# RWKV scan on one core: the carried state taken as one 128-column product per pair of heads

## The reference, cut to what matters

```
def wkv7_scan(r, decay, k, v, a, b):
    def step(S, inp):
        r_t, w_t, k_t, v_t, a_t, b_t = inp
        sa = jnp.einsum('bhij,bhj->bhi', S, a_t)
        S = S * w_t[:, :, None, :] + sa[..., None] * b_t[:, :, None, :] + v_t[..., None] * k_t[:, :, None, :]
        return S, jnp.einsum('bhij,bhj->bhi', S, r_t)
    ...
    _, y = lax.scan(step, S0, xs)
```

## Time and profile before

| what | value |
|---|---|
| runs (median, lowest, highest) | 2038.86, 2037.39, 2039.52 us |
| profiled execution, span | 2038.2 us (the page gives no other time of its own for it) |
| TensorE busy | 1990.5 us, 98% |
| VectorE busy | 1508.5 us, 74% |
| ScalarE busy | 1085.9 us, 53% |
| GpSimd busy | 164.5 us, 8% |
| DMA | 353.08 MB, mean 173 GB/s |
| chain that ended last | PE 77%, DVE 15%, ACT 4%, issue 2%, POOL 1% |
| mean granted TensorE clock | 0.991 |

### The profile page before, as it was taken

One profiled execution on the slowest core, in us unless ns is written; L12 is line 12 of the kernel. 1 busy time (PEld: TensorE's weight loads), 2 busy tenths in 40 slices (PEclk: granted clock), 3 DMA queues, 4 the chain that ended last, 5 costly groups with the idle time before them and its releaser, 6 DMA issues.

```text
span 2038.2 us, 33778 instructions
## 1 busy us (share of the span) xinstructions
PE 1990.5 (98%) x13448; PEld 1807.6 (89%) x13448; DVE 1508.5 (74%) x2550; ACT 1085.9 (53%) x1669; POOL 164.5 (8%) x92
## 2 busy tenths in 40 slices
PE   8999999999999999899999999999999999999999
PEld 7998879889888998689988779999999999888888
DVE  6776984777666775877756977899899996555555
ACT  6654832366555665666645665545544445555554
POOL 0000022300010000210001013232000000000000
PEclk9999998999999999899999999999999999999999
DMA  6566421256655666246566335546544446656664
GB/s 209 198 207 205 137 84 53 94 182 201 206 187 182 201 204 191 75 155 205 198 202 216 121 132 189 175 160 205 176 149 152 146 151 202 206 200 203 206 200 162
DMA packets 98172, 353.08 MB, mean 173 GB/s; under 512 B 10976, under 2 KB 12896, under 8 KB 97504
## 3 DMA queue, kind: packets, MB, share of 16 engines
q1 hardware_dynamic: 98016, 350.91, 52.1%
HBM read 349.82 MB, written 1.05 MB: 172 GB/s over the span
## 4 chain that ended last, share of the span: by engine, by line
PE 77%; DVE 15%; ACT 4%; issue 2%; POOL 1%; DMA 0%; SPq 0%; DVEq 0%; ACTq 0%
PE psum L312 16%; PE psum L314 16%; PE psum L313 16%; PE psum L326 15%; PE psum L327 7%; DVE tile_low L219 4%; ACT tile_high L207 1%; PE psum L956 1%; DVE peer_active L3133 1%; PE psum L1035 1%; PE psum L418 1%; DVE peer_onehot L3124 1%; PE psum L2846 1%; PE psum L1155 1%; POOL small L1790 1%
## 5 line engine op out<-in xcount | busy, mean ns | idle before, releaser
L219 DVE TENSOR_TENSOR tile_low<-raw_tiles,tile_high 128x1024 fp32r<-128x1024 f32 x608 | 752.5, 1240 | 346.6 <-ACT tile_high L207 346.1
L207 ACT ACTIVATE tile_high<-raw_tiles 128x1024 fp32r<-128x1024 f32 x642 | 675.0, 1053 | 393.6 <-PE psum L314 389.0
L326 PE MATMUL psum<-hT,tile_high 128*128 128x512 f32 x1408 | 463.5, 383 | 3.4 <-DVE hT L564 1.9
L327 PE MATMUL psum<-hT,tile_low 128*128 128x256 f32 x1408 | 383.8, 273 | 0.0
L312 PE MATMUL psum<-hT,tile_high 128*128 128x256 f32 x1152 | 324.9, 282 | 3.8 <-DVE tile_low L219 3.4
L314 PE MATMUL psum<-hT,tile_low 128*128 128x256 f32 x1152 | 317.6, 276 | 0.0
L313 PE MATMUL psum<-hT,tile_high 128*128 128x256 f32 x1152 | 317.5, 276 | 0.0
L312 PE MATMUL psum<-tile_high,hT 128*128 128x512 f32 (+1 forms) x816 | 312.0, 382 | 4.2 <-DVE tile_low L219 2.5
L313 PE MATMUL psum<-tile_low,hT 128*128 128x512 f32 (+1 forms) x816 | 308.4, 378 | 0.0
L314 PE MATMUL psum<-tile_high,hT 128*128 128x512 f32 (+1 forms) x816 | 308.2, 378 | 0.0
L326 PEld LDWEIGHTS psum<-hT,tile_high 128*128 128x128 f32 x1408 | 266.1, 189 | 41.0 <-DVE hT L564 2.1
(11 more groups left out here) (365 smaller groups left out, 2520.5 us busy)
## 6 DMA issues: line engine op xcount, KB each, us to landing
raw_tiles<-ffn_in_dram SPq DMA_DIRECT2D x176, 512.0 KB, 4.3
raw_tiles<-peer_u_dram SPq DMA_DIRECT2D x128, 512.0 KB, 3.4
raw_tiles<-peer_v_dram SPq DMA_DIRECT2D x128, 512.0 KB, 3.9
raw_tiles<-ffn_out_dram SPq DMA_DIRECT2D x88, 512.0 KB, 4.3
raw_tiles<-w_kv_dram SPq DMA_DIRECT2D x16, 512.0 KB, 4.1
raw_tiles<-in_gates_dram SPq DMA_DIRECT2D x16, 512.0 KB, 3.2
raw_tiles<-peer_q_dram SPq DMA_DIRECT2D x16, 512.0 KB, 4.3
raw_tiles<-w_k_dram SPq DMA_DIRECT2D x8, 512.0 KB, 4.3
```

Source lines behind the costliest of these rows:

```text
L207: scalar.activation(k.high[:, n % SLOTS, :], k.raw[:, n % RAW_SLOTS, :], ACT.Copy).then_inc(*k.tile_high_made.mark(n))
L219: vector.tensor_tensor(k.low[:, n % SLOTS, :], k.raw[:, n % RAW_SLOTS, :], k.high[:, n % SLOTS, :].bitcast(F32), ALU.subtract).then_inc(*k ...
L326: k.tensor.matmul(both_sums, high[:, c, :], both, start=(c == 0), stop=(c == KC - 1), skip_group_check=True)
L327: ins = k.tensor.matmul(both_sums[:, 0], low[:, c, :], both[:, 0], start=False, stop=(c == KC - 1), skip_group_check=True)
```

## The change

The helper `carried` goes. In its place `add_carried` issues, for a half, four products of 128 columns where `add` issued eight of 64. One product takes the 128x128 operand of a pair once and passes both heads' columns of `S0` through it. Since the rows of the other head are zero in each head's columns, as they were before, the sums are the same ones. It is called at four places: `w(1, 0)`, `w(1, 1)`, `y_known(1, 0)` and `y_known(1, 1)`.

```diff
-    def carried(rows, tb):
-
-        return lambda n: (r[rows][:, n // 2, block(tb)], head_of(r["S0"], n))
+    def add_carried(ps, half, rows, tb, first=False):
+
+        for c in range(4 * half, 4 * half + 4):
+            at = 2 * HD * (c - 4 * half)
+            tensor.matmul(ps[:, at:at + 2 * HD], r[rows][:, c, block(tb)], r["S0"][:, 2 * HD * c:2 * HD * (c + 1)],
+                          start=(first and c == 4 * half), stop=False, skip_group_check=True)
...
-            add(ps, half, carried("a_s", tb), first=True)
+            add_carried(ps, half, "a_s", tb, first=True)
...
-            add(ps, half, carried("r_s", tb))
+            add_carried(ps, half, "r_s", tb)
```

## The result

The changed kernel takes 2043.92 us (median of 12 runs, 2041.49 to 2045.65), the kernel before beside it 2038.9 (12 runs, 2037.21 to 2041.08). The ratio is 1.0024, with a 95% interval of 1.0016 to 1.0033: 16 products fewer, and 5.0 us more. The profiled execution has a span of 2042.9 us.

A forecast was written before the change was run, and what follows sets the result against it. VectorE's norm chain was taken to bound the stretch, so the shorter TensorE stream gains 0; half clock adds +0.7, +3.2 and +0.6, sum +4.5 us on 2038.86, giving 2043.4 us, range 2038.2 to 2045.6.

The forecast's parts named there:

- What bounds the stretch: From 355.76 us to the first transpose at 378.19, VectorE's masks, weight tiles and norm end the wait, not TensorE.
- The gain on the path: Time won ahead of the first transpose by the shorter TensorE stream: 0 us, bounds 0 and 3.6.
- The price of 128 columns: In the four widened groups, an instruction of 128 columns costs 0.112 us like one of 64, saving 3.6 us on TensorE.
- columns: In the widened groups, 128 columns cost double and TensorE saves 0 us; chance 0.05.
- The fall of the clock: TensorE idles 4.1 us ahead of the transposes, and its granted clock then falls to 0.50.
- Rival 1: After the hole the clock does not fall, or only outside work on the chain: 2038.9 us; chance 0.12.
- Its length: How long the clock stays at 0.50 behind the hole: about 378 to 388 us, other bound 3.4 us.
- rival 5: Half clock lasts through the second transposes: +6 to +7.5 us, 2045 to 2046.4; chance 0.07.
- the long case: Half clock from about 378 to 388 us, behind the hole, with small products there; chance 0.60.
- The transposes: The 8 transposes behind the hole, 1.16 us up to y, slow at half clock: +0.7 us.
- `y` of block 1: Its 32 instructions behind the transposes cost 0.217 instead of 0.112 us each at half clock: taken at +3.2 us.
- The `w_o` products up to the second transposes: 18 products beside the norm's chain, five at half clock, less 0.48 us to spare: +0.6 us, bounds 0 and 3.3.

The follow-up runs named there:

- a hole of 2.6 us: The kernel before with 0 instead of 18 identity products ahead of the transposes, nothing widened: 2043.03 us, ratio 1.0026.
- `y` in the hole: The changed kernel with TensorE computing y of block 1 ahead of the transposes of block 0, 18 identity products kept: 2038.01 us, ratio 0.9993.
- the two reordered kernels: y of block 1 ahead of the transposes of block 0: on the changed kernel 2038.01 us; on the kernel before, without identity products, 2037.71 us.
- the last two kernels: The kernel with the squares first timed again, 2037.62 us, and the same with 20 identity products filling the hole near 256 us, 2036.23 us.
- the kernel with the squares first: The reordered changed kernel, with ScalarE squaring y of block 1 before splitting transposed y of block 0, VectorE following: 2036.79 us, again 2037.62 us.

## Why the prediction was right, point by point

- **What bounds the stretch.** VectorE's chain, 19.9 us from the tiles to the transposes, kept its length, and the hole's releaser stayed. The gain on the path, taken at 0 us, was 0.
- **The price of 128 columns.** Taken at 0.112 us for an instruction, from six of 128 columns and 32 of 16 elsewhere in the program. Measured: eight from a start at 356.23 to the next group's at 357.18, 0.12 each with the seam, and 3.5 us saved of the 3.6 expected. The hole, expected at 4.1 us, is 4.03. The other bound, 128 columns at double the price and nothing saved (columns, given 0.05), is out.
- **The fall of the clock.** Taken as the likeliest, since the hole of 4.1 us was to be longer than any between two products before (the longest is 2.48 us) and the clock had been at 0.50 behind two of 2.4 and 2.5 us; it fell. Rival 1 is out: filling the hole took the loss away, and making it without the change brought the loss. In its favour stood a wait of 1.89 us that passed. The same trace also has a wait of 1.84 us (860.29 to 862.13) with 0.50 from 863.17, and one of 1.54 us (1177.66 to 1179.20) with 0.50 from 1180.61, so rival 1 had less for it than the prediction says.
- **Its length.** Taken at 10 us because small products follow; it was 13.65, in the direction of rival 5, but it ended 1.3 us before the second transposes. The reason given does not hold, so that the long case came is in part luck: at the short fall from 259.01 stand 64 instructions with outputs of 64 rows by 128 columns (L1035, 258.26 to 263.73), small ones too, and the clock was back after 3.4 us. What sets the length stays open.
- **The terms.** The transposes: +0.7 expected, and 1.77 us to `y` instead of 1.16, +0.6. `y` of block 1: +3.2 expected; 378.50 to the first `w_o` product at 385.19 is 6.69, before 3.49 (379.35 to 382.84), +3.2. The `w_o` products up to the second transposes: +0.6 expected; 385.19 to 391.70 is 6.51, before 4.62 (382.84 to 387.46), +1.9. This term was mis-sized: I put five of the 18 at half clock, and it was 12 of them (the twelfth starts at 390.02), 12 x 0.21 - 0.48 = 2.0. Sum +5.7 in this trace, against 4.5. The mechanism was right, and this is the term whose size was off.
- **The total.** +5.7 less the 1.4 us that the earlier hole happened not to cost makes 4.3; the spans differ by 4.7, so 0.4 lies elsewhere. Over the runs the difference is 5.0 us, between the 4.5 of the sum and the 5.7 of the trace; 2043.4 was said, 2043.92 measured. That the total came so near with its third term too small by 1.3 us is luck: the interval of the ratio leaves the difference anywhere from 3.3 to 6.7 us. Slower by over 0.2% was given 0.55, and the ratio is 1.0024, its interval still reaching below 1.002.

Of the expectations of the experiments these did not come true: spared executions at a hole of 2.6 us, of which the times show none; 2.6 us of gain for `y` in the hole, of which the medians show 0.8 and the trace 2.1; 0.9 us between the two reordered kernels, which the medians do not show; and, for the last two kernels, 2036.8 again and a narrower scatter.

## What to carry to other kernels

Before shortening a stream, look at who ends the wait behind it: where another engine does, the saving becomes idle time (3.5 us here, and the hole went from 0.49 to 4.03 us), and on TensorE idle time had a price here where the clock fell, paid by whatever stood next on the path (`y` of block 1 took 6.93 us instead of 3.68). Filling products are sized for one hole and have to be sized again when the work ahead of them changes (18 products left a hole of 0.49 us before, and it took 51 to leave 0.43 after the change; 40, which left 1.62, did as well in the times). Work of the path put into the hole did as well (2038.01 us against 2038.8), with the 18 products left as they were. And where fp32 products with a stationary operand each are issued one by one, one instruction of 128 columns cost here what one of 16 did: 0.12 and 0.11 us.

## What the runs showed of the hardware that had not been expected

After the hole the clock stayed low for 13.65 us in both traces, longer than any fall in the kernel before (10.2 us), though TensorE had hardly a break: it was busy for 13.63 of the 13.65 us in the changed kernel. For 6.7 of them it was at the 64-column products of `y`, for the last 5.2 at `w_o` products of 512 columns.

Not every fall had a hole ahead of it. The one of 10.2 us at 317.04 came after a stretch of the kernel before in which TensorE was busy all the time at full clock (columns as in the earlier trace rows):

```profile
303.10:317.03 13.93, 13.93 (x182) 12.48 (x182) 0.00 (x0) 4.05 (x6) 6.15 (x4) 1.00 0.57 206
```

From 311.45 on these were products of 32x32 and of 64 columns. A fall of this length stands near there in all ten traces, from 314.3 us at the earliest to 317.6 at the latest.

Nor did the length of a hole decide alone. The same hole of 2.4 us at the same place of the program was followed by a fall in four traces of nine, which makes 1.4 us of difference from one execution to another that no instruction of the kernel explains; the two traces of the kernel with the squares first differ in it (4.09 and 5.47 us). The hole of 2.48 us that ends at 1347.45 in the kernel before was followed by one in nine of ten traces, that of 1.89 us in two of ten, and at that of 1.84 us ahead of 862.13 the clock fell in all ten. What decides is not shown here.
